# Two layers of a hybrid block: token lists inside the shared expert's chunks, layer 1's shared products contraction-outermost, index work and branches in another order

## The reference

```
def swiglu(t, wg, wu, wd):
    return (jax.nn.silu(t @ wg) * (t @ wu)) @ wd

def grouped_moe(h, router_w, router_bias, w_gate, w_up, w_down, sh_gate, sh_up, sh_down):
    t = h.reshape(-1, shp[-1])
    scores = jax.nn.sigmoid((t @ router_w).astype(jnp.float32))
    ...
    _, g_idx = lax.top_k(group_score, TOPK_GROUPS)
    ...
    _, e_idx = lax.top_k(cand, TOP_K)
    w = jnp.take_along_axis(scores, e_idx, axis=-1)
    w = w / w.sum(-1, keepdims=True)
    ...
    out = swiglu(t, sh_gate, sh_up, sh_down)
    for e in range(N_EXPERTS):
        out = out + combine[:, e:e + 1] * swiglu(t, w_gate[e], w_up[e], w_down[e])
    return out.reshape(shp)
```

## Time and profile before

| | |
|---|---|
| median of 3 runs | 1476.88 us (1474.13 to 1477.4) |
| profiled execution, its own time | 1475.81 us |
| its span in the profile | 1474.0 us |
| TensorE busy | 1372.2 us, 93% |
| VectorE, ScalarE, GpSimd busy | 597.1, 394.7, 154.1 us |
| moved | 334.50 MB, mean 227 GB/s |

### The profile page before, as it was taken

The page is one execution under the profiler, slowest core; times in us unless marked ns, Lnnn a source line. Parts: engine busy times, 40 slices in busy tenths (PEclk is TensorE's granted clock), DMA queues, the critical chain, the costliest instruction groups (busy, mean ns, idle before and its releaser), DMA issues.

```text
span 1474.0 us, 29270 instructions
## 1 busy us (share of the span) xinstructions
PE 1372.2 (93%) x12461; PEld 840.3 (57%) x12461; DVE 597.1 (41%) x1095; ACT 394.7 (27%) x979; POOL 154.1 (10%) x182
## 2 busy tenths in 40 slices
PE   5999899999998999998999999999999999999876
PEld 2344444454444588754666666688757766655432
DVE  4365667456453756461222212242363532221112
ACT  2322343433434200311222222222152302221111
POOL 0000113032222200000111111000000001111100
PEclk9999999999999999999999999999999999999988
DMA  9554345334330633417999999967321369999993
GB/s 352 200 185 171 114 143 172 125 134 143 125 133 29 162 95 113 176 57 239 339 380 383 386 381 380 356 238 240 107 79 55 107 246 391 392 394 398 401 405 149
DMA packets 131495, 334.50 MB, mean 227 GB/s; under 512 B 13283, under 2 KB 63259, under 8 KB 125211
## 3 DMA queue, kind: packets, MB, share of 16 engines
q1 hardware_dynamic: 121851, 309.18, 57.7%
q0 software_dynamic: 6208, 12.60, 2.5%
q10 hardware_dynamic: 3296, 10.73, 2.0%
HBM read 325.79 MB, written 14.81 MB: 231 GB/s over the span
## 4 chain that ended last, share of the span: by engine, by line
PE 68%; SPq 17%; DMA 5%; DVE 5%; issue 3%; ACT 2%; POOL 0%; ACTq 0%; DVEq 0%; POOLq 0%
SPq L614 11%; PE ps L1277 11%; PE ps L1637 9%; PE ps L1294 8%; PE ps L1530 6%; PE ps L1676 5%; PE ps L1587 5%; SPq L616 4%; DMA ring<-in_moe_w_down 3%; PE ps L1219 2%; PE ps L1956 2%; PE ps L1698 2%; PE ps L1866 2%; PE ps L1371 2%; PE ps L1899 1%
## 5 line engine op out<-in xcount | busy, mean ns | idle before, releaser
L1277 PE MATMUL ps<-aT,ring 128*128 128x512 f32 x384 | 174.9, 603 | 2.2 <-issue 2.2
L1637 PE MATMUL ps<-ring,ssb 128*32 128x256 f32 x2256 | 136.6, 387 | 9.2 <-DMA ring<-in_moe_w_up 7.2
L2480 DVE COPY big<-ps 32x256 f32<-32x256 f32 x162 | 68.6, 423 | 145.6 <-PE ps L1676 143.8
L1637 PE MATMUL ps<-tmp,ssb 128*32 128x256 f32 x1984 | 117.9, 384 | 8.1 <-DMA tmp<-in_moe_w_up 8.1
L2471 DVE TENSOR_TENSOR ssb<-ssb,ps 128x128 f32<-128x128 f32 (+1 forms) x56 | 19.1, 347 | 259.8 <-ACT ssb L1039 258.6
L1277 PEld LDWEIGHTS ps<-aT,ring 128*128 128x128 f32 x384 | 70.7, 192 | 85.5 <-issue 83.1
L1637 PEld LDWEIGHTS ps<-ring,ssb 128*32 128x32 f32 x2256 | 87.2, 112 | 52.9 <-DMA ring<-in_moe_w_up 13.6
L1294 PE MATMUL ps<-aT,ring 128*128 128x512 f32 x256 | 114.7, 597 | 0.0
L1676 PE MATMUL ps<-ring,ssb 128*32 128x256 f32 x1648 | 96.7, 386 | 3.7 <-DMA ring<-in_moe_w_down 3.1
L1637 PEld LDWEIGHTS ps<-tmp,ssb 128*32 128x32 f32 x1984 | 69.9, 111 | 52.2 <-issue 8.5
L1052 ACT COPY big<-ps 32x256 f32<-32x256 f32 x162 | 58.7, 362 | 141.2 <-PE ps L1676 139.6
(11 more groups left out here) (438 smaller groups left out, 1955.6 us busy)
## 6 DMA issues: line engine op xcount, KB each, us to landing
ring<-in_ada_w SPq DMA_DIRECT2D x44, 1024.0 KB
ring<-in_moe_w_down SPq DMA_DIRECT2D x40, 1024.0 KB
ring<-in_moe_w_gate SPq DMA_DIRECT2D x56, 512.0 KB
ring<-in_moe_w_up SPq DMA_DIRECT2D x56, 512.0 KB
tmp<-in_moe_w_gate SPq DMA_DIRECT2D x48, 512.0 KB
tmp<-in_moe_w_up SPq DMA_DIRECT2D x48, 512.0 KB
ring<-in_ssd_in_w SPq DMA_DIRECT2D x20, 1024.0 KB
tmp<-in_moe_w_down SPq DMA_DIRECT2D x16, 1024.0 KB
```

Source lines behind the costliest of these rows:

```text
L1277: ins = pe.matmul(ps[:, bank, :], slot(u)[:, k, (i % 2) * P:(i % 2 + 1) * P], aT[:, k, :], start=(k == 0), stop=(k == KD - 1))
L1637: ins = pe.matmul(tiled_gu[32 * c:32 * c + 32, 2 * h + i, :].rearrange("p (r n) -> p r n", r=2), XgT[l][:, k * C + 32 * g:k * C + 32 * g + ...
L2480: ins = dve.tensor_copy(Y[s % 2][32 * g:32 * g + 32, 256 * c:256 * c + 256], tiled_y[32 * c:32 * c + 32, 2 * h + i, :])
```

## The change

It has five parts.

- Layer 0, TensorE: ranks and counts stand inside shared chunk 1, between its gate and up halves, and the lists inside chunk 2.
- Layer 1, TensorE: the four chunks are replaced by `hidden_rows`: slice k is the outer loop, and for each slice come four products for chunks 0 and 2 (g = 0) and four for chunks 1 and 3 (g = 1), in four banks at once. The router's small products stand between these groups of four. The four shared weight units are now released one by one, and silu and multiply take two chunks at once (`two_chunks`).
- VectorE: `route` is cut; the pairs' weights (`pair_weights`) go ahead of chunk 0's eviction in layer 0 and to the end in layer 1. The operations on order and flag (`order_and_flag`) go ahead of the one-hot matrices in layer 0, and behind the indices in layer 1. The six evictions of layer 1 are reordered, so that two banks come free first.
- The last eviction stands behind the branch on VectorE and ScalarE (in layer 1 two of four chunks), and on ScalarE in layer 0 behind the copy of the gathered rows.
- SyncE: the first permuted unit no longer waits for the indices where its slot is held, as in layer 1.

```
-                    if s == AHEAD_EXPERTS[l] and j == 0 or u.slot not in held:
+                    if u.slot not in held:
                         sp_.wait_ge(s_gi, 3 * l + 3)
...
+                def two_chunks(g):
+                    act.wait_ge(s_gu[1], KF)
+                    act.activation(sg[g][:, :], ps[:, 2 * g, :], ACT.Silu).then_inc(s_sg[1], 2)
...
+                def hidden_rows(beside):
+
+                    order = [(0, 0), (1, 0), (0, 1), (1, 1)] + [(k, g) for k in range(2, KD) for g in range(2)]
+                    for i, (k, g) in enumerate(order):
+                        if g == 0:
+                            if k % 2 == 0:
+                                dense_arrived(0, k // 2)
+                            pe.wait_ge(s_a, parts_to(3) + k + 1)
+                        elif k == 0:
+                            pe.wait_ge(s_fc, 2)
+                        for f in (g, g + 2):
+                            for r in range(2):
+                                ins = pe.matmul(ps[:, 2 * g + r, f // 2 * n:f // 2 * n + n],
+                                                pair_slot(unit(0, k // 2))[:, k % 2, r, f * P:(f + 1) * P], aT[:, k, 0:n],
+                                                start=(k == 0 and f == g), stop=(k == KD - 1), skip_group_check=True)
+                        if k % 2 and g:
+                            ins.then_inc(s_gu[1], 1)
+                        for work in beside.get(i, ()):
+                            work()
...
+                if l == 0:
+                    hidden_chunk(0, 0)
+                    token_rows(0, 2 * nt)
+                    hidden_chunk(0, 1, ranks_and_counts)
+                    hidden_chunk(0, 2, row_lists)
+                    hidden_chunk(0, 3)
+                else:
+                    hidden_rows({2: [logit_parts], 3: [logit_sums], 4: [lambda: token_rows(0, 2)], 5: [lambda: token_rows(2, 4)],
+                                 6: [ranks_and_counts], 10: [row_lists]})
...
-                chunk(0, 0)
-                chunk(0, 1)
-                place(l)
-                chunk(0, 2)
-                indices(l)
-                chunk(0, 3)
+                if l == 0:
+                    pair_weights(0)
+                    chunk(0, 0)
+                    place(0)
+                    chunk(0, 1)
+                    indices(0)
+                    chunk(0, 2)
+                else:
+                    place(1)
+                    indices(1)
+                    order_and_flag(1)
+                    pair_weights(1)
                 dense = spread(dve, l)
+                if l:
+                    two_chunks(0)
                 with dve.If(dense):
...
                 with dve.Else():
+                    if l == 0:
+                        chunk(0, 3)
                     rowsT_dve(l, 0)
+                    if l:
+                        two_chunks(1)
                     for s in range(NE):
                         tiled_dve(l, s)
```

More of the change, by code:

```diff
@@ L1078, in moe_act @@
                 act.dma_start(m_rows[0:n, :].rearrange("(t p) n -> p t n", p=P), mtok[:, 0:nt, :]).then_inc(s_mr, 16)
-                for f in range(1, KF):
+                for f in range(1, KF - 1 if l == 0 else 1):
                     chunk(0, f)
                 sparse = choose(act, l)
+                if l:
+                    two_chunks(0)
                 with act.If(sparse):
@@ L1103, in moe_act @@
                 with act.Else():
+                    if l == 0:
+                        chunk(0, KF - 1)
+                    if l:
+                        two_chunks(1)
                     for e in range(1, NE + 1):
@@ L1546, in logit_parts @@
                         pe.wait_ge(s_fc, 6)
+                        pe.wait_ge(s_a, parts_to(3) + KD)
                     for k in range(KD):
@@ L1565, in dense_arrived, with hidden_chunk @@
                     pe.wait_ge(s_w[u.slot], u.arrived + (loaded_again(l, u) if e else 0))
-                def hidden_chunk(e, f):
+                def hidden_chunk(e, f, between=None):
                     q = KF * e + f
@@ L1579, in hidden_chunk @@
                         for r in range(2):
+                            if r and between:
+                                between()
                             if l == 0 and q == 0 and h == 0 and r == 1:
@@ L1766, in moe_pe @@
-                pe.wait_ge(s_sel, l + 1)
-                sel = [rts[l][12][:, t * NE:(t + 1) * NE] for t in range(nt)]
-                for t in range(nt):
-                    for q in range(t + 1):
-                        pe.matmul(ps[:, 6, t * NE:(t + 1) * NE], tri_f if q == t else ones[:, :], sel[q],
-                                  start=(q == 0), stop=(q == t))
-                for q in range(nt):
-                    ins = pe.matmul(ps[:, 6, 64:64 + NE], ones[:, :], sel[q], start=(q == 0), stop=(q == nt - 1))
@@ new lines, in token_rows, with ranks_and_counts @@
+                def token_rows(first, last):
+                    for r in range(first, last):
+                        if r >= 2:
+                            pe.wait_ge(s_mtv, 8 * l + r - 1)
+                        for k in range(4):
+                            kk = 4 * (r % 2) + k
+                            ins = pe.transpose(ps[:, (4, 7)[r % 2], k * P:(k + 1) * P], aT[:, kk, (r // 2) * P:(r // 2 + 1) * P], ident)
+                        ins.then_inc(s_mt8, 1)
+                def ranks_and_counts():
+                    pe.wait_ge(s_sel, l + 1)
+                    for t in range(nt):
+                        for q in range(t + 1):
+                            pe.matmul(ps[:, 6, t * NE:(t + 1) * NE], tri_f if q == t else ones[:, :], sel[q],
+                                      start=(q == 0), stop=(q == t))
+                    for q in range(nt):
+                        ins = pe.matmul(ps[:, 6, 64:64 + NE], ones[:, :], sel[q], start=(q == 0), stop=(q == nt - 1))
+                    ins.then_inc(s_rl, 1)
@@ new lines, in row_lists @@
+                def row_lists():
+                    pe.wait_ge(s_oh, 4 * l + nt)
+                    pe.wait_ge(s_val, 18 * l + 18)
+                    for e in range(NE):
+                        for t in range(nt):
+                            ins = pe.matmul(ps[0:C, 5, 3 * e:3 * e + 3], onehot[l][:, t, e, 0:C], val[l][:, t, e, :],
+                                            start=(t == 0), stop=(t == nt - 1))
+                    ins.then_inc(s_rl, 1)
+                if l == 0:
[7 more added lines that the diff above has]
+                                 6: [ranks_and_counts], 10: [row_lists]})
@@ L2429, in place, with order_and_flag @@
                                        rank1[l].unsqueeze(2).to_broadcast([P, NE, NE]), ALU.is_equal))
+                if l == 0:
+                    order_and_flag(0)
+                for t in range(nt):
+                    dve.tensor_tensor(onehot[l][:, t, :, 0:C], iota1[:, 0:C].unsqueeze(1).to_broadcast([P, NE, C]),
+                                      rank[l][:, t * NE:(t + 1) * NE].unsqueeze(2).to_broadcast([P, NE, C]), ALU.is_equal)\
+                        .then_inc(s_oh, 1)
+            def order_and_flag(l):
+                count = ps[:, 6, 64:64 + NE]
                 link(dve.tensor_tensor(pprod[l], permT[l], erev[:, 0:NE].unsqueeze(1).to_broadcast([P, NE, NE]), ALU.mult))
```

64 lines of the change are left out of this document (35 added, 29 removed).

## The result

The changed kernel takes 1468.25 us (median of 5 runs, 1466.52 to 1470.95), the kernel before 1475.08 (5 runs, 1474.05 to 1477.4). Of the 5.6 us between forecast and result, 1.8 are the level: the forecast stood on a median of 1476.88 for the kernel before, and with two more runs that median is 1475.08. The ratio on record is 0.9939, 95% interval 0.9925 to 0.9953. The profiled execution took 1468.45 with a span of 1466.7, 7.3 us less than the span before.

The account below looks back on a forecast made before the run. TensorE was taken to lead the first expert stage, with transfers close behind, and DMA to limit the second. Layer 0's 2.0 us plus layer 1's 1.1 gave 3.1 us saved, to 1473.8 us; range 1470.0 to 1478.0.

Parts of the forecast that it names:

- Layer 0, the lists inside the chunks: Layer 0's shared chunks: same sum of products, last one still ends near 681.1; ranks 6.9 us earlier, indices some 8.
- the 0.65 us of cover: Layer 0: TensorE reaches the lists after 13.86 us, VectorE's chain to the one-hots takes 13.2; the forecast took 0.
- The handover: Layer 0, last shared product to first expert product: 1.90 us instead of 5.67, so TensorE starts 3.8 us earlier.
- The clock's 2.6 us: Layer 0's first 96 expert products: 2.6 us more gained if the clock doesn't fall after the short handover; 6.4 in all.
- What DMA lets through: First expert stage: of TensorE's 3.8 to 6.4 us, weight transfers follow by only 2.0 us; bounds 0 and 5.1.
- The signs that it gave for the cap: First expert stage: DMA share near 1.03 in 722 to 778; TensorE's transfer waits between 840 and 925 3 us or more.
- DMA doesn't follow: Rival, layer 0: the last-landing engine had no idle time, head start becomes waiting; 1 to 2 us saved; chance 0.29.
- DMA follows TensorE entirely: Rival, layer 0: the whole 3.8 to 6.4 us, plus 1.1, is 4.9 to 7.5 us saved; chance 0.2.
- Layer 1: Layer 1, selection to first permuted transfer: it goes out at 1189.7 instead of 1190.78, 1.1 us gained; bounds 0.3 and 2.0.
- its end moves with its start: Second expert stage: a weight stream at the DMA limit, so the 1.1 us earlier start counts at the end.
- the slower rival: Layer 1: the gather lands late among the weights and DMA runs dry; some 4 us slower, at 1481; chance 0.09.
- the full-follow case: Rival with transfers following TensorE wholly in layer 0: 1469.4 to 1472.0 us, chance 0.2; the range leaves out half.

Follow-up runs that it names:

- e3: Kernel before with only layer 0's branches of ScalarE and VectorE ahead of their last evictions, ranks and lists between whole chunks; ratio to before 0.9949.
- e4: Kernel before with only layer 0's ranks and lists inside the chunks, branches behind the last evictions as before; ratio to before 1.0009.
- e9: Kernel before plus five throwaway products on TensorE, fitted into the idle time of layer 0's handover; ratio to before 0.9963.
- e1: Changed kernel with every edit of layer 1 put back, so only the layer 0 part is left; ratio to before 0.9953.
- e10: Changed kernel plus one throwaway product ahead of TensorE's waits for weights in layer 1's last three experts; ratio to before 0.9930.
- e7: Changed kernel with layer 1's order and flag computed ahead of the indices instead of behind them; ratio to before 0.9925.
- e11: e7 with SyncE's first permuted transfer held until the gather's indices stand; ratio to before 0.9914.
- e2: Changed kernel with layer 0 put back, so only the layer 1 part is left; ratio to before 0.9995.
- e12: e7 with SyncE's wait for all indices as before the change, plus e10's throwaway products; ratio to before 0.9921.

## Why the prediction was wrong, step by step

**Layer 0, the lists inside the chunks.** Right. The last shared product ended at 680.86; the 0.65 us of cover held. e3 and e4 show no effect of this part that can be told; up to about 1 us isn't excluded (see e3).

**The handover.** Right: 1.92 us against 1.90. The clock's 2.6 us came as well (5.39 us against 5.37), and e9 shows that they come from TensorE being busy.

**What DMA lets through.** This is the step that failed. I took 2.0 us of the 6.4; the chip gave all of it. Stage 0 is 6.9 us shorter (e1: 7.3), a little more than TensorE's head start of 6.6. The text had named its own refutation, "if layer 0's end moves by the whole 4 to 6 us", and it moved by 7.2. The signs that it gave for the cap failed too: the share of 722 to 778 did rise (0.99 to 1.01), but TensorE's waits for transfers between 840 and 925 fell to nothing instead of growing to 3 us. Two readings in it were wrong.
First, I counted idle time by the share of busy DMA engines: (1.03 - 0.98) x 40, (1.03 - 0.91) x 20 and (1.03 - 0.97) x 16, over 1.03, which is 5.1 us in all and 3.2 without the first. The bytes stood in the same rows. Against the 385 GB/s of 778 to 838 they give (385 - 354)/385 x 40 = 3.2, (385 - 313)/385 x 20 = 3.7 and (385 - 352)/385 x 16 = 1.4, together 8.3 us. That is more than 6.4, so by bytes the transfers could follow. The share is the time that packets took, and a packet took longer while the stream was thin: in 722 to 742 packets of 4 KB took 189 ns on average, in 778 to 838 they took 173. So the share was 12% below full there and the bytes 19%. The Trainium skill (Perfetto Trace Analysis, Identifying the Most-Contended Engine) has a sentence that I hadn't weighed: for DMA the occupancy is misleading, and HBM utilization, thus what is moved, is to be read instead. The runs agree: the change used 6.9 us, more than the 5.1 that the share leaves. The 8.3 are no sharp limit, though: 385 GB/s is itself not the most that was moved (the kernel before has 401 in 742 to 762), and against 401 the same three windows leave 11 us. No run shows where the limit lies.
Second, I set aside the first 40 us because four units are tied to 681.1. They are, but TensorE doesn't need them at once. The stream behind them waits for slots that TensorE frees. SyncE's waits in the kernel before, 682 to 722, say so, 26.0 of 40 us:

```profile
SPq L614 <- PE ps L1637: 20.6, 8, 6.0
SPq L616 <- PE ps L1676: 5.4, 2, 3.2
```

In the changed kernel 390 instead of 354 GB/s were moved there. The wait of 1.0 us in the earlier trace rows was no sign of a limit either: in kernels with the same changed layer 0 it is nothing in one and 0.8 us in another.
The rival "DMA doesn't follow" (0.29) leaned on that wait and on two slower engines of the 16. The length of stage 0 refutes it; no view here names single engines. The rival "DMA follows TensorE entirely" is what happened, at 0.2 and with 4.9 to 7.5 us: the spans differ by 7.3.

**Layer 1.** The working was right to 0.2 us at each point. Counted with the 7.16 us of lead added, VectorE went on at 1174.9 (predicted 1174.9), lists ended at 1182.7 (1182.6), indices at 1185.9 (1185.7), the flag stood at 1188.3 (1188.3) and the first permuted transfer went out at 1189.8 (1189.7). The term was right as a start and wrong as a gain: "its end moves with its start" left out the tail, where TensorE waits for transfers and its clock is low. 1.0 us went in at the front, 0.8 were left where the last gate and up unit is used, and 0.1 came out behind the down products. The layer 1 lengths agree (316.0, 316.5 and 317.3 against 316.2 to 316.8), though they scatter by more than the term, and e10 shows that the tail's clock is worth such an amount; that it is the whole reason was not separated from the slow first microseconds of the stream (below). The late gather that the slower rival feared didn't come in the changed kernel (5.13 us), but it did in e7 and e11 (8.3 and 8.2 us), where it stopped the gain halfway.

**The sum.** 6.4 + 1.1 = 7.5 us would have given 1469.4 on the level of the medians. All the terms were in the text; the wrong choice was to cap one of them. That 7.5 is so near the 7.3 us of the spans is in part luck: layer 0 gave 7.2 instead of 6.4, layer 1 0.1 instead of 1.1. The cap also set the range too high: its lower end left out half of the full-follow case, which I had priced at 1469.4 to 1472.0.

## What to carry to other kernels

Before a gain is capped by the DMA engines, read the GB/s of each window against the GB/s of a full one, not the share of busy time, and ask what the stream waits for: if it is slots that the faster engine frees, it follows. Put a branch beside work that is already queued on another engine, and never between an eviction and the engine that waits for it; moved alone, this gave 6.2 of the 6.9 us of layer 0's stage here, and the finer reordering of layer 0 gave nothing that could be told. After a front has been moved, look at the clock in the last stage: a stream's end may come earlier without the work behind it.

## What the runs showed of the hardware that was not expected

- The time of issue behind VectorE's branch in layer 0 was 3.67 (before), 3.62 (e9), 6.05 (e2) and 6.79 us (e4) in four kernels in which it stood at the same place. TensorE's time of issue at its branch in layer 1 was 2.9 us in e12, and nothing in layer 0.
- A gather of rows in layer 1 landed after 4.9 to 6.7 us where the first weights went out with it (within 0.1 us) or behind it, and after 8.2 to 8.3 us where they had gone out 0.56 or 1.2 us ahead of it.
- In the changed kernel, which issues both within 0.1 us, the DMA share fell to 0.51 over 1186 to 1188; the kernel before had 0.87 in the matching 2 us (1194 to 1196), with as many transfers of weights issued, five at the start of either.
- Behind ranks and counts of layer 0 one shared chunk of 32 products took 15.53 us instead of 13.84 in 13 of the 14 kernels, in the changed one with a granted clock of 0.89 over 636 to 652 (0.58 over 644 to 648, behind 3.0 us of products of 16 columns, and 1.00 around it); e3's trace, with the same small products, stays at 1.00. Why is open.
